# Order of products inside a weight tile, and a later turning of dt, in a single-core hybrid block

## What is computed

```python
zxbcdt = x @ w_in                                   # state space: z, x, B, C and dt
dt = jax.nn.softplus(dt_raw + dt_bias)
da = (dt * a); da_cum = jnp.cumsum(da, axis=-1)     # per token and head
y = _ssd_chunked(xs, dt, a, bm, cm) + xs * d_skip
...
o = o * jax.nn.silu(gate); return o @ w_out         # gate: half of x @ b_w_in
...
a = jax.nn.relu(h @ w1); return (a * a) @ w2        # MLP
```

## Time and profile before

| | |
|---|---|
| median of three runs | 2135.53 us (2134.35 to 2138.06) |
| profiled execution, its time | 2134.09 us |
| profiled execution, span | 2132.3 us |
| TensorE busy | 2116.2 us, 99% |
| TensorE weight loads busy | 1780.5 us, 84% (they overlap the matmuls) |
| VectorE busy | 1394.5 us, 65% |
| ScalarE busy | 1146.8 us, 54% |
| DMA | 399.24 MB, mean 187 GB/s |
| TensorE's granted clock | full (1.00) but for the first 9.7 us and the end |

### The profile page before, as it was taken

How to read it: one execution, slowest core, us unless ns; L and a number is a source line. 1 busy time by engine, 2 the same in 40 slices (tenths; PEclk the granted TensorE clock), 3 DMA queues, 4 the chain that set the end, 5 groups by cost and what they waited for, 6 DMA issues and landing times.

```text
span 2132.3 us, 28331 instructions
## 1 busy us (share of the span) xinstructions
PE 2116.2 (99%) x11037; PEld 1780.5 (84%) x11037; DVE 1394.5 (65%) x2206; ACT 1146.8 (54%) x1943; POOL 18.4 (1%) x30
## 2 busy tenths in 40 slices
PE   8999999999999999999999999999999999999999
PEld 7888888888887878888788888888888888888887
DVE  6988888887555887765845555556664445565453
ACT  5666667676434556643745666544444334444332
POOL 0000000000000000000000000000000000000000
PEclk9999999999999999999999999999999999999999
DMA  7655666656675644466566554456666666665664
GB/s 270 198 188 188 192 194 189 189 176 197 219 236 162 208 148 129 160 206 188 172 218 190 182 172 152 149 180 188 190 191 191 194 196 185 185 187 188 196 211 134
DMA packets 109622, 399.24 MB, mean 187 GB/s; under 512 B 12128, under 2 KB 12512, under 8 KB 108848
## 3 DMA queue, kind: packets, MB, share of 16 engines
q1 hardware_dynamic: 105552, 378.73, 56.8%
q0 software_dynamic: 3936, 18.70, 2.4%
HBM read 395.21 MB, written 2.16 MB: 186 GB/s over the span
## 4 chain that ended last, share of the span: by engine, by line
PE 95%; DVE 3%; ACT 1%; DMA 0%; issue 0%; SPq 0%; ACTq 0%; DVEq 0%
PE ps L1479 93%; PE ps L1482 2%; DVE wlo L878 1%; ACT lnt L574 0%; DMA raw<-in_w_in 0%; ACT whi L577 0%; DVE xs L887 0%; DVE xhl L878 0%; DVE small L884 0%; DVE d L887 0%; ACT xhl L577 0%; DVE res L887 0%; SPq L507 0%; DVE sms L881 0%; DVE sms L878 0%
## 5 line engine op out<-in xcount | busy, mean ns | idle before, releaser
L878 DVE TENSOR_TENSOR wlo<-raw,whi 128x1024 fp32r<-128x1024 f32 (+1 forms) x713 | 869.1, 1222 | 605.9 <-ACT whi L577 604.3
L577 ACT ACTIVATE whi<-raw 128x1024 fp32r<-128x1024 f32 (+1 forms) x713 | 753.1, 1058 | 927.3 <-PE ps L1479 910.2
L1479 PE MATMUL ps<-xhl,whi 128*128 128x512 f32 (+1 forms) x2568 | 905.2, 398 | 5.7 <-ACT whi L577 4.7
L1479 PE MATMUL ps<-xhl,wlo 128*128 128x256 f32 x2560 | 715.3, 280 | 0.6 <-DVE wlo L878 0.6
L1479 PEld LDWEIGHTS ps<-xhl,whi 128*128 128x128 f32 x2568 | 482.9, 189 | 124.2 <-ACT whi L577 4.7
L1479 PEld LDWEIGHTS ps<-xhl,wlo 128*128 128x128 f32 x2560 | 483.0, 189 | 1.2 <-DVE wlo L878 1.2
L1479 PE MATMUL ps<-whi,xhl 128*128 128x512 f32 x1088 | 349.0, 397 | 3.2 <-ACT xhl L577 2.5
L1479 PEld LDWEIGHTS ps<-whi,xhl 128*128 128x128 f32 x1088 | 202.9, 188 | 53.7 <-ACT xhl L577 6.1
L1479 PE MATMUL ps<-wlo,xhl 128*128 128x512 f32 x544 | 208.2, 390 | 0.0
L1479 PE MATMUL ps<-whi,hhi 128*128 128x512 f32 x512 | 199.2, 389 | 0.0
L1479 PE MATMUL ps<-whi,hlo 128*128 128x512 f32 x512 | 199.2, 389 | 0.0
(11 more groups left out here) (199 smaller groups left out, 1807.1 us busy)
## 6 DMA issues: line engine op xcount, KB each, us to landing
raw<-in_w SPq DMA_DIRECT2D x256, 512.0 KB, 3.7
raw<-in_w_in SPq DMA_DIRECT2D x159, 512.0 KB, 3.6
raw<-in_w_qkv SPq DMA_DIRECT2D x96, 512.0 KB, 3.6
raw<-in_w_ao SPq DMA_DIRECT2D x64, 512.0 KB, 4.2
raw<-in_w_bi SPq DMA_DIRECT2D x32, 512.0 KB, 3.6
raw<-in_w_gate SPq DMA_DIRECT2D x32, 512.0 KB, 3.5
raw<-in_w_bo SPq DMA_DIRECT2D x32, 512.0 KB, 4.3
raw<-in_w_o SPq DMA_DIRECT2D x32, 512.0 KB, 3.5
```

Of the source, the lines that this page charges most:

```text
L577: return eng.activation(out, x, ACT.Copy, **kw)
L878: return eng.tensor_tensor(out, x, y, op)
L1479: return eng.matmul(out, x, y, start=start, stop=stop, skip_group_check=True)
```

## The change

Three things are changed. In a unit by features (but for the first tile) the products of a tile stand in another order: the eight high-weight ones, then the eight low-weight ones, where before they alternated. They are the same 16 products on the same banks. The turning of dt to tokens comes one visit later on TensorE and VectorE, and with it the scan of group 0 (`scan_at(0)`, from 21 to 22). ScalarE's copy of unit n's sums waits for its own tanh of unit n - 2, which stands ahead of it in its queue. In the diff the pieces stand in this order: `plan`, `scan_at`, ScalarE's `in_proj`, and `time_steps` on VectorE and on TensorE.

```diff
         if units[u].feat:
-            order = [(b, p) for p in range(3) for b in range(2)] if i == 0 else [(b, p) for b in range(2) for p in (3, 2)]
-            visits.append((i, None, [(i, 4 * j + h, b, p) for h in range(4) for b, p in order]))
+            if i == 0:
+                products = [(i, h, b, p) for h in range(4) for p in range(3) for b in range(2)]
+            else:
+                products = [(i, 4 * j + h, b, p) for p in (3, 2) for h in range(4) for b in range(2)]
+            visits.append((i, None, products))
...
 def scan_at(g):
-    return ended("in", ORDER.index((g, "x3")) // 2) + (8 if g else 10)
+    return ended("in", ORDER.index((g, "x3")) // 2) + (8 if g else 11)
...
             def in_proj(n):
                 yield
                 w.wait_ge(S["conv"], convs_before[max(n - 1, 0)])
+                w.wait_ge(S["tanh"], 2 * (n - 1))
...
                 ts2(acol[:, :], ones[0:64, :], al, ALU.mult, -1.0, ALU.mult).then_inc(S["dt"], 1)
-                yield
+                yield 2
                 w.wait_ge(S["dt_t"], 1)
...
                 q.then_inc(S["dt_in"], 1)
-                yield 7
+                yield 8
                 dt = d64[7]
```

## The result

The changed kernel took 2129.9 us (median of six runs, 2129.44 to 2130.47), the kernel before 2137.8 us in its six (2134.35 to 2140.27). The ratio is 0.9964, with a 95% interval of 0.9951 to 0.9977: faster by 0.36%, where 0.8% was forecast. The profiled execution took 2130.12 us.

A forecast was written before the change was run, and what follows sets the result against it. TensorE's own start-to-start time was taken as the bound; 16.0 us (order) + 0.9 (`wlo` waits) + 0.6 (`acol` wait) = 17.5 us took 2134.09 to 2116.6, plus 1.4 for the median: 2118.0 us, range 2109 to 2134.5.

The forecast's parts named there:

- What bounds the kernel: Whole kernel: TensorE, busy 2116 of 2132.3 us, sets the pace; DMA, ScalarE and VectorE don't.
- What a pair costs before: Units by features: a 512- and a 256-column product take 0.3463 or 0.3534 us, mean 0.3506, a tile 2.805 us.
- the median is 1.4 us above that time: Final sum: 1.4 us added to the profiled execution's forecast 2116.6 us, giving 2118.0 us.
- I take 0.1168 us: Short products in the new order: 0.1168 us each, borrowed from dt's run of 32 products of 256 columns.
- the surcharge at most once: New tile order: about 7 ns extra once a tile, where one length gives way to the other; tile 2.755 us.
- So alternating lengths carries a surcharge: Old order in units by features: alternating long and short products costs an estimated 7 ns a pair above separate runs.
- Rival (a): Tiles by features: short product 0.1196 us, only the upper level's extra goes; gain 12.7 us, 2122.8 us; chance 0.22.
- Rival (b): Tiles by features: short products at 0.1134 us, half the long step; gain 26.1 us, 2109.4 us; chance 0.10.
- Rival (c): Tiles by features: new order falls into as dear a steady pattern; only 1.5 us go, 2134.0 us; chance 0.14.
- Rival (d): Tiles by features: wide loads don't hide behind short runs, 0.1239 us or more each; 5.5 us slower, 2141.0 us; chance 0.10.
- Low weights later, and dt: Waits for `wlo` at slots 1 and 2 go, 0.9 us; the transposes' wait for `acol` goes, 0.6 us.
- the nearer scan of group 1: Scan of group 1, 17 visits on instead of 18: costed at 0, up to 1 us if a wait reaches TensorE.

The follow-up runs named there:

- dt alone: All of the change but the new order of products (later dt with the scan, ScalarE's tanh wait), against the kernel before: 2138.62 us, ratio 1.0004.
- The series: Separate kernels running only bare TensorE products, nothing else active; total time means nothing. Steps 0.2268 us (512 columns, 128 wide), 0.1200 (256, 128 wide).

## Why the prediction was wrong in size

**What bounds the kernel: right.** TensorE's own steps were all there was to win, and side work, weights and DMA stayed out of it.

**What a pair costs before: right for the trace, but not for the kernel.** The two levels were read from the earlier trace rows and taken as a property of stretches of the program. They are a state that the products ahead leave: in the trace of dt alone the same stretch, with the same order, had the other level. The mean of 2.805 us a tile came within 2 ns for the profiled execution (the differences by stages give 2.803), which had more tiles at the cheap level than that trace, and the step "the median is 1.4 us above that time" rested on a median of three runs. With six runs the median was 3.7 us above.

**The step that failed: "I take 0.1168 us, since dt's run is the nearest row in columns, number form and length of run, and since half of its loads are as wide."** It measured 0.120 us. Half of dt's loads being narrow was the very thing that made the row too cheap: 0.120 wide and 0.113 narrow. Over eight products and 319 tiles this is 8.2 us. The second term, "the surcharge at most once", 7 ns a tile, measured 20 ns: 4.1 us more. Together a tile is 2.793 us instead of 2.755, 12.2 us less to gain; 17.5 - 12.2 = 5.3 us would have been the gain from the profiled execution, and 4.0 came. Of the rest 0.5 us is the late first product, and some 0.7 us the mean before, read 2 ns a tile too high.

**The step ahead of it failed with it: "So alternating lengths carries a surcharge".** It compared the two levels with 0.2267 + 0.1168 us. With the measured 0.120 the sum is 0.3467 us, exactly the cheap level: there alternating costs nothing extra, and at the dear level 6.7 ns a pair. Runs of eight cost 20 ns a tile themselves. So the change didn't take a surcharge away; it put one of 20 ns a tile in place of 0 or 53, whichever level the tile had stood at. Against a kernel at the cheap level throughout it would, by these numbers, be a loss; no version at that level throughout was found.

**Rival (a) had the right price** for the short product, 0.1196 us, from the cheap level taken as the plain sum of both. It lacked the surcharge at the change, and so gave 2122.8 us. **Rival (b)** fell with 0.113 us only under narrow loads. **Rival (c)**, "a product costs by its place in whatever steady pattern the array falls into", had the mechanism but not the size: the new order is a steady pattern of its own, but not one "as dear"; it is dearer than the cheap level of before and cheaper than the dear one. **Rival (d)** fell: 0.120 us is below 0.1239, and a run of 16 has the same.

**Low weights later, and dt: right.** Both waits for `wlo` and the one for `acol` went, 0.9 and 0.6 us in the trace. dt alone shows no gain in the times (ratio 1.0004); 0.5 us is too little for them to show. The wait for tanh and the nearer scan of group 1 cost nothing that the trace shows.

**The range** held the result by its width, not by its reasons, which is luck: the case held likeliest, 2113 to 2122 us, was 8 us off. The measured 7.9 us are also twice what the two profiled executions differ by, 4.0, since the one of before happened to be a short one.

Still open is what inside TensorE makes the 13.3 ns, the 20 ns at a change and the two levels. The series show that it is not other engines, not the pace of loads alone, not a debt, and not banks; a fixed beat against which starts fall would fit levels 6.7 ns a pair apart that hold for good, but no run shows such a beat by itself.

## What to carry to other kernels

Before a stream's step is borrowed from another stretch of the trace, compare all that a product has, its load's width too; a bare series of the very products would have given 0.120 us and the 20 ns at each change. When the runs of a kernel differ by several microseconds at full clock and one trace shows two paces for one and the same code, take the distribution as part of what is to be predicted: here half of the measured gain is absent from the two profiled executions, and what explains it best is that the new order has one pace where the old had two. The trace of dt alone, in which the old order stood at the dear level more often, shows all of it. An order that sets its own pace in each tile, such as runs of two or runs that meet across tiles, is worth more than one that is cheap only behind the right neighbour.

## What the runs showed of the hardware that was not expected

TensorE's step for fp32r products with a new 128-wide operand each was 226.7, 173.3 and 120.0 ns for 512, 384 and 256 columns, 13.3 ns above the columns at 2.4 GHz. Products of 224 and 128 columns both took 112 ns. An alternating series of 512 and 256 columns runs for good at 346.7 or at 353.3 ns a pair, as the products ahead leave it (five and 19 of 24 series); the dearer is a cycle of three pairs of 349, 350 and 361 ns. And 512 columns under a 64-wide operand took 230 ns, more than under a 128-wide one.
